# First norm as products with a diagonal; vectors turned later; attention of the first head three steps later

## The reference

```python
h = rms_norm(x, norm_mix_w[l], NORM_EPS)        # x * rsqrt(mean(x*x) + eps) * w
proj = h @ w_in[l]
q, k, v, z, xbc, dt_raw, gate_a, gate_s = jnp.split(proj, split_at, axis=-1)
q = apply_rotary(q.reshape(b, s, ATT_HEADS, 2, ATT_HEAD_DIM), cos, sin)   # k likewise
att = diff_attention(q, k, v, lam)              # softmax(c=0) - lam * softmax(c=1), 8 heads
ssd = ssd_branch(z, xbc, dt_raw, ...)           # a scan over chunks of 128 tokens
x = x + (sigmoid(gate_a) * (att @ w_a) + sigmoid(gate_s) * (ssd @ w_s)) @ w_out
x = x + hierarchical_moe(rms_norm(x, norm_ffn_w), ...)   # 64 experts, the 2 best for each token
```

## Time and profile before

| | |
|---|---|
| median of the runs | 2467.88 us (2467.82 to 2468.67) |
| profiled execution, its own time | 2466.94 us |
| its span | 2465.7 us |
| PE busy | 2249.9 us, 91% |
| DVE, ACT, POOL busy | 936.1, 701.5, 585.5 us |
| DMA | 575.46 MB, mean 233 GB/s |

### The profile page before, as it was taken

One profiled execution on the slowest core, in us unless ns is written; L12 is line 12 of the kernel. 1 busy time (PEld: TensorE's weight loads), 2 busy tenths in 40 slices (PEclk: granted clock), 3 DMA queues, 4 the chain that ended last, 5 costly groups with the idle time before them and its releaser, 6 DMA issues.

```text
span 2465.7 us, 32513 instructions
## 1 busy us (share of the span) xinstructions
PE 2249.9 (91%) x13122; PEld 1659.2 (67%) x13122; DVE 936.1 (38%) x1817; ACT 701.5 (28%) x1379; POOL 585.5 (24%) x685
## 2 busy tenths in 40 slices
PE   7999999999999989988888778788879999999999
PEld 5776888988888565554444444444447857888887
DVE  5677677776322241110000000000127575542441
ACT  4545556565221010000000000000014475331330
POOL 4443577775100111111111111111104160000000
PEclk9999999999999999999999999999999999999999
DMA  7322243443436489999999999999983212122220
GB/s 188 99 79 73 86 143 97 122 135 129 180 114 263 157 345 425 425 427 426 426 426 426 426 426 427 427 426 426 427 322 133 86 36 69 69 103 103 103 102 36
DMA packets 149593, 575.46 MB, mean 233 GB/s; under 512 B 14972, under 2 KB 75928, under 8 KB 124736
## 3 DMA queue, kind: packets, MB, share of 16 engines
q1 hardware_dynamic: 127728, 534.77, 54.7%
q0 software_dynamic: 16288, 28.98, 3.5%
q10 hardware_dynamic: 5424, 9.58, 1.5%
HBM read 562.69 MB, written 31.52 MB: 241 GB/s over the span
## 4 chain that ended last, share of the span: by engine, by line
PE 59%; DMA 28%; DVE 6%; ACT 3%; issue 3%; POOL 2%; ACTq 0%; DVEq 0%; SPq 0%; POOLq 0%
PE ps L689 14%; PE ps L691 13%; PE ps L690 13%; DMA ringx<-in_w_expert_gate 7%; DMA ringx<-in_w_expert_up 6%; PE ps L1051 6%; DMA ring<-in_w_expert_up 4%; DMA ring<-in_w_expert_gate 4%; PE ps L1081 3%; PE ps L953 2%; PE ps L682 2%; DMA ringx<-in_w_expert_down 2%; DMA ringy<-in_w_expert_gate 2%; DMA ringy<-in_w_expert_up 1%; PE ps L794 1%
## 5 line engine op out<-in xcount | busy, mean ns | idle before, releaser
L2312 DVE TENSOR_TENSOR hid<-ps,sg 128x256 f32<-128x256 f32 x64 | 27.2, 425 | 823.6 <-issue 808.3
L689 PE MATMUL ps<-hTh,hb 128*128 128x512 f32 x576 | 237.0, 411 | 3.0 <-DVE ringr L1883 3.0
L1051 PE MATMUL ps<-ringx,gxT 128*64 128x256 f32 x1664 | 200.4, 392 | 40.6 <-DMA ringx<-in_w_expert_up 25.4
L691 PE MATMUL ps<-hTh,ringr 128*128 128x512 f32 x576 | 226.1, 393 | 0.0
L690 PE MATMUL ps<-hTl,hb 128*128 128x512 f32 x576 | 225.1, 391 | 0.0
L1674 ACT COPY ys<-ps 128x512 f32<-128x512 f32 x64 | 37.5, 586 | 621.8 <-PE ps L1081 621.8
L1051 PEld LDWEIGHTS ps<-ringx,gxT 128*64 128x64 f32 x1664 | 135.0, 135 | 113.8 <-issue 66.0
L2734 POOL DMA_INDIRECT gx<-h2d,rows x64 | 65.7, 1027 | 507.1 <-PE ps L682 441.7
L1883 DVE TENSOR_TENSOR ringr<-ring,hb 128x1024 fp32r<-128x1024 f32 x112 | 147.8, 1321 | 89.8 <-ACT hb L1400 89.1
L1051 PE MATMUL ps<-ring,gxT 128*64 128x256 f32 x1216 | 145.7, 390 | 29.5 <-DMA ring<-in_w_expert_up 18.7
L1051 PE MATMUL ps<-ringy,gxT 128*64 128x256 f32 x1216 | 145.3, 390 | 27.6 <-DMA ringy<-in_w_expert_up 17.5
(11 more groups left out here) (458 smaller groups left out, 4641.5 us busy)
## 6 DMA issues: line engine op xcount, KB each, us to landing
ringx<-in_w_expert_gate SPq DMA_DIRECT2D x26, 2048.0 KB, 45.6
ringx<-in_w_expert_up SPq DMA_DIRECT2D x26, 2048.0 KB, 46.0
ringx<-in_w_expert_down SPq DMA_DIRECT2D x25, 2048.0 KB, 46.0
ring<-in_w_expert_down SPq DMA_DIRECT2D x19, 2048.0 KB, 46.1
ring<-in_w_expert_gate SPq DMA_DIRECT2D x19, 2048.0 KB, 45.6
ring<-in_w_expert_up SPq DMA_DIRECT2D x19, 2048.0 KB, 46.1
ringy<-in_w_expert_down SPq DMA_DIRECT2D x19, 2048.0 KB, 46.2
ringy<-in_w_expert_gate SPq DMA_DIRECT2D x19, 2048.0 KB, 45.6
```

Source lines behind the costliest of these rows:

```text
L689: pe.matmul(o, lh, rh, start=start and n == 0, stop=False)
L691: m = pe.matmul(o, ll, rh, start=False, stop=stop and n == len(ks_) - 1)
L1051: m = pe.matmul(b[c * 64:c * 64 + 64, 0:256].rearrange("p (n j) -> p n j", j=2), gxTs[e % 2][:, k % 4, k // 4 * 64:k // 4 * 64 + 64], w4[: ...
```

## The change

The scaled copy `XN` goes. DVE scales the identity by the roots of a tile (`Ws[0]`, a diagonal of 128x128), and PE multiplies `X` by it: the product is the turned tile times its roots. All tiles of a slice `k` lie side by side in bank `k`. The norm's weight is loaded as 8x128, turned by one PE operation into eight columns of `st`, and applied when the slices leave PSUM: ACT writes `hTh` with it as scale, DVE `hTl`. Both go slice by slice over all 512 tokens, after the first two weight blocks are cast, and the first projection waits for each slice by itself. The positions are loaded after the third root. The small vectors are turned at the fifth step of the second head, and the loop gives three head steps alone before attention begins, on all engines.

```diff
+def heads_beside():
+    for n in range(3):
+        yield 0, n
+    for side, n in merged(46, 28):
+        yield side, n if side else n + 3
...
-    nrow_mix = over("nrow", [128, D], F32, work0 + 65152)
+    nrow_mix = over("nrow", [8, 128], F32, work0 + 65152)
+    squares = over("squares", [128, NT, D], F32, region_a + 32768)
...
     def pe_start():
         pe.wait_ge(*at("ident", 16))
+        pe.wait_ge(*at("nrow", 16))
+        pe.transpose(banks[7][:, 384:392], nrow_mix[:, :], ident[0:8, 0:8]).then_inc(s["nmT"], 1)
         for tt in range(NT):
             pe.wait_ge(*at("xn", tt + 1))
-            for i in range(2):
-                b = bank(2 * tt + i)
-                pe_turn4(b, lambda k: XN[:, tt, (i * 4 + k) * 128:(i * 4 + k) * 128 + 128]).then_inc(s["xT"], 1)
-                held[2 * tt + i] = at("htl", 2 * tt + i + 1)
-        pe.wait_ge(*at("htl", 8))
+            if tt == NT - 1:
+                pe.wait_ge(*at("nmc", 1))
+            ts = slice(tt * 128, tt * 128 + 128)
+            for k in range(8):
+                m = pe.matmul(banks[k][:, ts], X[:, tt, k * 128:k * 128 + 128], Ws[0][:, ts], start=True, stop=True)
+                if tt == NT - 1:
+                    m.then_inc(s["xT"], 1)
+                    held[k] = at("htl", k + 1)
...
     def pe_proj(n, part):
+        for k in range(part * 4, part * 4 + 4):
+            if n == 0:
+                pe.wait_ge(*at("htl", k + 1))
...
-        pe_vectors()
-        for side, n in merged(49, 28):
+        for side, n in heads_beside():
             if side == 0:
                 pe_head(1 + n // 7, n % 7)
+                if n == 4:
+                    pe_vectors()
...
     def act_start():
-        a.dma_start(nrow_mix[:, :], t["norm_mix_w"].to_broadcast([128, D])).then_inc(s["nrow"], 16)
-        for n in range(NT + 2):
-            if n < NT:
-                a.wait_ge(*at(f"xa{n}", 16))
-                a.activation(XN[:, n, :], X[:, n, :], ACT.Square, scale=1.0 / 32,
-                             accum_out=st[:, 8 + n:9 + n]).then_inc(s[f"ssq{n}"], 1)
-            if n > 1:
-                tt = n - 2
-                for i in range(2):
-                    a.wait_ge(*at("xT", 2 * tt + i + 1))
-                    a.copy(hTh[:, i * 4:i * 4 + 4, tt * 128:tt * 128 + 128],
-                           banks[2 * tt + i][:, :].rearrange("p (k c) -> p k c", k=4)).then_inc(s["hth"], 1)
-        for n in range(3):
+        a.dma_start(nrow_mix[:, :], t["norm_mix_w"].rearrange("a (r c) -> (a r) c", c=128)).then_inc(s["nrow"], 16)
+        for n in range(NT):
+            a.wait_ge(*at(f"xa{n}", 16))
+            a.activation(squares[:, n, :], X[:, n, :], ACT.Square, scale=1.0 / 32,
+                         accum_out=st[:, 8 + n:9 + n]).then_inc(s[f"ssq{n}"], 1)
+        for n in range(2):
             act_hi(n)
+        a.wait_ge(*at("nmc", 1))
+        for k in range(8):
+            a.wait_ge(*at("xT", k + 1))
+            a.activation(hTh[:, k, :], banks[k][:, :], ACT.Copy, scale=st[:, 104 + k:105 + k]).then_inc(s["hth"], 1)
+        act_hi(2)
...
     def dve_start():
+        v.wait_ge(*at("nmT", 1))
+        v.tensor_copy(st[:, 104:112], banks[7][:, 384:392]).then_inc(s["nmc"], 1)
+        for tt in range(NT):
+            v.wait_ge(*at("rs1", tt + 1))
+            v.tensor_scalar(Ws[0][:, tt * 128:tt * 128 + 128], ident, st[:, 12 + tt:13 + tt], None, MUL).then_inc(s["xn"], 1)
         for n in range(2):
             dve_lo(n)
+        for k in range(8):
+            v.wait_ge(*at("hth", k + 1))
+            v.scalar_tensor_tensor(hTl[:, k, :], banks[k][:, :], st[:, 104 + k:105 + k], hTh[:, k, :], MUL,
+                                   SUB).then_inc(s["htl"], 1)
...
     def pool_first():
-        g.dma_start(posi[:, :], t["positions"].to_broadcast([128, S])).then_inc(s["posi"], 16)
         g.wait_ge(*at("ident", 16))
         for tt in range(NT):
             g.wait_ge(*at(f"ssq{tt}", 1))
             pool_rstd(st[:, 12 + tt:13 + tt], st[:, 8 + tt:9 + tt], 1e-6, "rs1")
+            if tt == 2:
+                g.dma_start(posi[:, :], t["positions"].to_broadcast([128, S])).then_inc(s["posi"], 16)
```

More of the change, by code:

```diff
@@ L197 @@
 ONCE = (
-    ("once_v", ("lam", "vcol", "vcols", "wdl", "dts", "dtm", "da", "wrt", "rex", "rw", "AS", "nov", "rank", "idx",
+    ("once_v", ("nmc", "lam", "vcol", "vcols", "wdl", "dts", "dtm", "da", "wrt", "rex", "rw", "AS", "nov", "rank", "idx",
               "inc", "ovn")),
     ("once_a", ("ssq0", "ssq1", "ssq2", "ssq3", "lame", "dtr", "dte", "ecm", "rexd", "rwd")),
-    ("once_pe", ("vt", "dtp", "dtt", "cum", "cnt", "rk", "blks")),
+    ("once_pe", ("nmT", "vt", "dtp", "dtt", "cum", "cnt", "rk", "blks")),
 )
@@ L273, in build @@
     hTl = sb("hTl", [128, 8, S], F32R)
-    XN = sb("XN", [128, NT, D])
+    PM.take([128, NT, D])
     hTh = sb("hTh", [128, 8, S], F32R)
@@ L717, in pe_proj @@
         lo = block_of(ringr[block_at(n)[0] % RING], n)
-        m = mm3(banks[n % 2][:, :], lambda k: (hbs[n % 4][:, k, :], lo[:, k, :]),
-                lambda k: (hTh[:, k, :], hTl[:, k, :]), range(part * 4, part * 4 + 4), part == 0, part == 1)
+        for k in range(part * 4, part * 4 + 4):
+            if n == 0:
+                pe.wait_ge(*at("htl", k + 1))
+            m = mm3(banks[n % 2][:, :], lambda k: (hbs[n % 4][:, k, :], lo[:, k, :]),
+                    lambda k: (hTh[:, k, :], hTl[:, k, :]), range(k, k + 1), k == 0, k == 7)
         if part:
@@ L1886, in dve_start @@
         v.wait_ge(*at("ident", 16))
[L1887 to L1898, removed]
+        v.wait_ge(*at("nmT", 1))
[3 more added lines that the diff above has]
+            v.tensor_scalar(Ws[0][:, tt * 128:tt * 128 + 128], ident, st[:, 12 + tt:13 + tt], None, MUL).then_inc(s["xn"], 1)
         for n in range(2):
             dve_lo(n)
+        v.wait_ge(*at("nmc", 1))
+        for k in range(8):
+            v.wait_ge(*at("hth", k + 1))
+            v.scalar_tensor_tensor(hTl[:, k, :], banks[k][:, :], st[:, 104 + k:105 + k], hTh[:, k, :], MUL,
+                                   SUB).then_inc(s["htl"], 1)
         v.wait_ge(*at("posi", 16))
@@ L2263, in dve_first @@
         dve_lambda()
-        dve_vectors()
-        for side, n in merged(49, 28):
+        v.wait_ge(*at("consts", 16))
+        for side, n in heads_beside():
             if side == 0:
                 dve_head(1 + n // 7, n % 7)
+                if n == 4:
+                    dve_vectors()
                 if n == 30:
```

## The result

| | before | after |
|---|---|---|
| median of the runs | 2468.16 us (2467.82 to 2471.35, 6 runs) | 2478.68 us (2475.63 to 2480.84, 6 runs) |
| profiled execution, span | 2466.94, 2465.7 us | 2476.18, 2474.9 us |

The ratio of after to before is 1.0036, with a 95% interval of 1.0026 to 1.0046: slower by 6 to 11 us. The forecast was 2464.5, with 2468.8 as its upper end. The change did save what was forecast at the start, and lost nearly four times as much between 44 and 270 us.

The account below looks back on a forecast made before the run. PE's progress up to about 890 us was taken as the bound, everything behind shifting with it. Start gain 3.85 less 0.5 us for later scores gave 3.35: 2467.9 to 2464.5 us, range 2460.8 to 2468.8.

Parts of the forecast that it names:

- DMA: Kernel start: 0.78 MB leave the queues ahead of X and the first weight block, taken as 2.0 us.
- roots: First norm on POOL: fourth root about 12.0 us, after X's last tile lands at 8.9 and an added 0.75 us issue.
- products: First norm on PE: 32 diagonal products start at 7.1 us, 11 at 0.42 and 21 at 0.225 us, end at 16.4.
- split: High and low parts on ACT and DVE: first projection at 17.3 us instead of 21.82, low parts done at 22.1.
- rival B: First norm's products stay at half clock, ending at 20.6 us; gain only 1.2 us, 2466.7 us; chance 0.12.
- The second chain: Sine, cosine, ACT copies to 40 us: raw copy 3 ends 40.1 instead of 40.74, PE's six microseconds shrink to net 3.85.
- rival E: Second chain doesn't bind because DMA lands earlier or casts slip in; PE keeps the whole 6 us, 2461.9; chance 0.09.
- ends of the unknown: Sums if sine starts at 21.0 us, 4.9 us, or at 24.2 us (rival B), 1.7 less 0.5.
- The wait for the keys' rotation just before 44.09 goes too: First head's scores, near 44 us: starting three steps later removes PE's wait for rotated keys; no size given.
- Scores three steps later: Attention loop: 28 attention steps over 46 head steps instead of 49, costing 0.5 us of PE waiting for softmax weights.
- rival C: Attention loop: steps denser than softmax latency allows, 7.1 us come back, 2471.2 us, slower; chance 0.16.
- Rival D: Near 1841 us: clock may stay up, 1.8 us more gained, 5.2 in all, 2462.7 us; chance 0.15.

Follow-up runs that it names:

- e10_swap2: Changed kernel, first attention step after three head steps, order of the kernel before again from the fourth attention step: 2463.51 us, ratio 0.9981.
- e1_lead0: Changed kernel without the lead, attention beginning as before (28 attention steps over 49 head steps), new norm and later vectors kept: 2468.16 us, ratio 0.9998.
- e2_only_lead: Kernel before with only the three head steps ahead of attention, old norm, vectors ahead of the loop: 2483.86 us, ratio 1.0059.
- e6_lag3: Changed kernel, lead of three kept, attention as thin as before (28 steps over 49 head steps): 2482.14 us, ratio 1.0056.
- e8_lead2: Changed kernel with two head steps ahead of attention instead of three: 2476.89 us, ratio 1.0034.
- the two late starts: Changed kernel, first attention steps one or two product steps later, then the order of the kernel before: 2464.77 and 2463.51 us.
- e4_thin_before: Kernel before with POOL rotating only 64 of 512 columns from the third head on: 2468.28 us, ratio 0.9994.
- e3_thin_after: Changed kernel with POOL rotating only 64 of 512 columns from the third head on: 2468.02 us, ratio 0.9997.

## Why the prediction was wrong

*DMA, roots, products, split: right, with some luck.* The first projection started at 17.14 us (forecast 17.3), sine at 21.52 (22.1), and the products ended at 16.4 us as forecast; rival B did not occur. Within that, the products began 0.3 us late and the clock rose about 1 us before the 11.7 us of the sum, after 7 or 8 slow products instead of 11, and the two nearly cancel. The fourth root came at 11.1 us instead of 12.0, since most of the DMA issue that was added for 0.75 us ran while POOL waited anyway; PE was busy with earlier tiles, so it cost nothing.

*The second chain: right.* The gain did shrink from six to about four microseconds at PE's waits for ACT's copies (1.2 and 1.3 us, 3 in all forecast). Raw copy 3 ended at 39.4 (forecast 40.1), and e10_swap2 measured the net gain at 3.78 us against 3.85. Of rival E no more than those 0.7 us were there. (The prediction's ends of the unknown mix two sums: 4.9 us leaves its 0.5 us for the scores out, 1.7 less 0.5 takes it in.)

*"The wait for the keys' rotation just before 44.09 goes too": right but unpriced.* In before PE's weight load stood 0.45 us for it; in e1_lead0, where PE's last product ahead of it comes 5.5 us earlier (38.2 against 43.7) and POOL's rotation ends only 1.5 us earlier, it is 4.05 us and the clock behind it. This is the one thing that the later start of the scores was worth.

*Scores three steps later: wrong, and the step that failed.* It was priced as "0.5 us of PE standing", because DVE, "which covers it", was busy 66% and 71%. The loss in that step was 14.6 us (10.8 + 3.85), and 15.5 us where it stood alone (e2_only_lead). The bulk of it is POOL's operations lying on DVE's, with the clock behind the waits: 10.7 us go with the thinned rotation, 10.4 at a lead of one with POOL held. 2.5 us are rival C. A busy share can't tell how long an instruction in the middle of the dependency chain takes. The same trace held the warning: L1965 on 128x128 had a mean of 849 ns where its shortest took 351, so before already met POOL there. A shift of the order decides anew which of DVE's operations meet POOL's six of 1.3 us per head, and before had a lucky draw: more low parts (1559 ns mean against 1216 undisturbed) and fewer weights. Leads of one, two and three all drew worse. The prediction walked the queues of PE, DVE and ACT, and never laid POOL's beside DVE's.

*Rival C: its sign showed, and its cause is a small part.* PE waits above 4 us for L1979 were named as its mark, and they came; but at the old density the loss stayed (e6_lag3). What density does own is the 2.53 us wait, which neither thinning nor holding POOL removes. It can be read from the written order. `merged(46, 28)` puts attention step 15 (from 0) behind step 14 with nothing between them but the head's empty step; `merged(49, 28)` has no such place. The lead of two has one, at step 7, and e6_lag3 one at its end, at step 27. In each the wait is there, to the hundredth, and the weights are at their short durations; the orders of before, of a lead of one and of the two late starts have no such pair and no such wait. PE at step 15 of thinned after, step 7 of e8_lead2 and step 27 of e6_lag3:

```profile
133.53 0.66 PE L790 MATMUL ps<-consts,bw 128*128 128x128 f32 x2 [2.53 <-DVE bw L1979]
```

```profile
83.48 0.41 PE L790 MATMUL ps<-consts,bw 128*128 128x128 f32 x2 [2.53 <-DVE bw L1979]
```

```profile
230.94 0.66 PE L791 MATMUL ps<-consts,bw 128*128 128x128 f32 x2 [2.53 <-DVE bw L1980]
```

In after the granted clock stayed at 1.00 behind it, so C is 2.5 us of the loss; in thinned after it was 0.57 from 133 to 137 us, which costs at most another 1.7 us there (an estimate: 0.43 of 4 us). The prediction looked for trouble between steps 1 and 2, where one half projection is left, and missed the place where none is. The chance given to slower, 0.08, was far too small, for each mechanism in the sum had been looked for on PE's side.

*Rival D: it happened, and was no cause.* In the profile of after the products stayed at full clock:

```profile
1852.67 0.23 PE ps L699
```

This gave back some 1.5 us (7 or more products at 0.43 in before), and the profiled executions, 9.2 us apart, differ by as much less than the router's 10.8. But e4_thin_before, with the order of before, also kept the clock there, and e10_swap2 lost it:

```profile
1839.14 0.43 PE ps L698
...
1841.70 0.43 PE ps L698
```

So this clock isn't tied to how early the stage comes. It may be a part of the scatter between runs of one kernel (2460.91 to 2466.97 us in e10_swap2); that wasn't tested.

## What to carry to other kernels

Before an order is shifted, look in the trace for forms whose mean is far above their minimum: another engine may be holding them already, which the timeline shows, and the shift draws anew who is held. Lay GpSimd's elementwise operations beside VectorE's on the critical chain by time, not by busy share. Read the written order, too, for two dependent steps with no product between them. Where a stall at one place is to be buried, move that one step and let the order fall back into its old phase, rather than shifting the whole loop.

## What the hardware showed

- Beside GpSimd's TENSOR_TENSOR on 128x512, some VectorE instructions wait for whole instructions, even tiny ones: a TENSOR_SCALAR on 128x2 took 1.23 us instead of 0.17 in e3_thin_after beside a full-width rotation. It goes both ways: in after a low part took 2.20 us (1.22 alone) and the rotation's operation beside it 2.25 us (1.3 alone).
- Others aren't held: beside such operations the TENSOR_SCALAR on 128x1 (L1977 in after) stayed at 0.21 us and the one that reads PSUM (L1983) at 0.34, and the RECIPROCAL on 128x2 was never over 0.17 us in any trace.
- The custom operation that reads scores from PSUM (L1966) kept its time beside POOL, 0.42 us on 128x256, with `consts` as its second input from SBUF. A custom operation with both inputs in SBUF (L1935, 128x64) didn't: 1.32 us beside POOL in e1_lead0, 0.22 alone in after.
- Behind some idle stretches of TensorE the granted clock fell, behind others it did not. In after it was 0.57 in the 4 us from 58, 198 and 256 us, right behind waits of 1.56, 3.25 and 2.25 us, and 1.00 in the 4 us from 84, 139 and 221 us, right behind waits of 1.93, 2.53 and 1.92. In e1_lead0 some 5 us of products ran at 0.63 instead of 0.39 us behind the wait of 4.05.
